# Router logits from unnormalised rows, inside the cross-attention output projection, with the norm factor taken per token

## Chip, cores and metric

One core of one Trainium2 chip. The metric is device microseconds of one execution. The kernel before was timed in three runs; its profile is of a fourth execution. Everything is float32 unless said otherwise.

## Reference

A model of two blocks on 256 tokens of width 1024. The first block is attention and a product-key retrieval of single-neuron experts; the second is convolution and a gated recurrence, cross attention over a memory, and a mixture of experts. The change touches the seam between the last two:

```python
x = x + memory_cross_attention(h, mem_n, w_q, w_k, w_v, w_o)   # ... @ w_o last
h = rms_norm(x, norm_ffn_g)          # x * rsqrt(mean(x*x) + EPS) * g
x = x + hierarchical_moe(h, ...)
return rms_norm(x, final_norm_g)

def hierarchical_moe(h, ...):
    group_probs = softmax(t @ w_group + b_group)         # 4 groups
    g_p, g_idx = top_k(group_probs, 1)
    e_logits = t @ w_expert + b_expert                   # 4 x 8 experts
    e_p, e_idx = top_k(softmax(e_logits of that group), 2)
    weights = g_p * e_p / sum(e_p)
    expert_ids = g_idx * 8 + e_idx
    for e in range(32):
        hid = silu(t @ w_gate[e]) * (t @ w_up[e])        # 1024 -> 512
        y = y + combine[:, e:e + 1] * (hid @ w_down[e])  # 512 -> 1024
```

## The kernel before, in words

The program is one long `build` with a block for each engine: TensorE (PE), VectorE (DVE), ScalarE (ACT), GpSimd (POOL), and the queue engine SP, which issues the loads. The order on each engine is the order of the code, and semaphores join them. x lies transposed as `Xv` (128 features x 8 blocks x 256 tokens). `TT` is 2 tiles of 128 tokens, `KT` 8 blocks of 128 features.

*Weights before the experts* stream through a ring of four slots, each a pair of 1024-column units (1 MB); SP loads pair n when pair n-4 is used (L409 to L423). `project` (L1186) makes one unit of output, 128 features x 256 tokens, from 8 matmuls of a 128x128 stationary tile and 256 streamed columns; each float32 matmul is two passes in the records. The eight units of the cross-attention output (`xo`, L1304) go to banks 0 to 3 in turn, and VectorE adds each to x (L1856, `x4_ready`).

*The router stretch* comes next. ScalarE squares each block of x (L790), PE sums them over features with a matrix of ones (L1308), ScalarE takes the root (L792), VectorE its reciprocal (L1860) and writes the normalised rows h into `Hv` (L1863). PE makes the logits, tokens on partitions, with h as the stationary tile and the 36 router columns streamed (L1315), then turns h and x to token-major form, one 128x128 block at a time (L1325); ScalarE copies the turned banks to `h_tok` and `x_tok` (L795). VectorE adds the bias (L1868), picks the group and two experts (L1869 to L1894), waits for ScalarE's two exponentials (L802, L803), makes the weights `w12` (L1898 to L1901), and one-hot rows `chosen` and `weight` over 32 experts (L1903 to L1911). PE counts each token's place among its expert's tokens (L1330 to L1334) and zeroes the four accumulator banks 0 to 3 by matmuls (L1340). VectorE computes the number of rounds, which every engine reads into a register (L1914 to L1922).

*The expert loop* has 16 pairs of experts a round; 64 slots for each expert; one round is enough when no expert has over 64 tokens. For each pair VectorE makes a one-hot selection `sel` (`one_hot`, L1925); PE gathers the rows of h by it (`gather`, L1344, 32 passes), ScalarE copies them (`take_gathered`, L813), PE does gate and up (`gate_up`, L1360, through `both`, L1357), then turns, down and, one pair later, `scatter` (L1369). The weights of a pair are 12.6 MB. Pair 0's are loaded during the second block (L416 to L420 and L445 to L447), the gates of pair 1 after the last `xo` unit (L449 to L451); from there SP waits for `gate_mm`, `up_mm` and `down_mm` of the pair before (L455 to L462), so each load starts when PE has used what its buffer held.

*The end*: after the last scatter VectorE adds x (L1970), ScalarE squares and roots, VectorE normalises (L1975), SP stores.

Of the kernel before, what the change touches and what calls it, by code (L numbers as in the profile page):

```python
# [19 lines left out]
ALU = mybir.AluOpType  # L20
# [4 lines left out]
P = 128  # L25
# [70 lines left out]
for _n, _w in (("b_mod", 48), ("norm1_g", 8), ("norm2_g", 8), ("final_norm_g", 8), ("norm_mix_g", 8),  # L96
# [16 lines left out]
    "squares_ready": (("sq1_ready", 2), ("sqg_ready", 5), ("sqo_ready", 2), ("sq2_ready", 8), ("sqm_ready", 1), ("sqx_ready", 8), ("sqh_ready", 2), ("sqc_ready", 1), ("sqn_ready", 8), ("sq5_ready", 8)),  # L113
    "deviation_ready": (("std1_ready", 1), ("stdg_ready", 3), ("stdo_ready", 2), ("std2_ready", 1), ("stdm_ready", 1), ("stdx_ready", 2), ("stdc_ready", 1), ("stdh_ready", 2), ("stdn_ready", 1), ("std5_ready", 1), ("std6_ready", 2)),
    "sums_ready": (("ss1_ready", 1), ("ssg_ready", 3), ("sso_ready", 2), ("ss2_ready", 1), ("ssm_ready", 1), ("ssx_ready", 1), ("meanc_ready", 1), ("varc_ready", 1), ("ssh_ready", 2), ("ssn_ready", 1), ("ss5_mm", 1)),
    "h_ready": (("h_x_ready", 8), ("H3_ready", 8), ("H4_ready", 8), ("H5_ready", 8)),
    "x_ready": (("x1_ready", 8), ("x2_ready", 8), ("x2n_ready", 8), ("x3_ready", 8), ("x4_ready", 8)),
# [14 lines left out]
def build(nc, t):  # L132

    ctx = ExitStack()
    with ctx:
# [174 lines left out]
        sq5, rs5 = three(area(4096, 2048), KT), area(6144, 256)  # L310
# [24 lines left out]
        ss5, ri5 = rr[:, 24:26], rr[:, 26:28]  # L335
        cmp4 = rr[:, 28:32]
# [52 lines left out]
        def _(sp):  # L389
# [19 lines left out]
            for m in range(RING, PAIRS2):  # L409
# [4 lines left out]
                if m in (6, 24, 26):  # L414

                    i = {6: 2, 24: 0, 26: 1}[m]  # L416
                    if m == 24:
                        second_done(sp, *BETWEEN[-1])
                    sp.dma_start(w_exp[0][:, 4096 * i:4096 * (i + 1)], t[("moe_gate", "moe_up", "moe_down")[i]][0]).then_inc(
                        S(("gates_in0", "ups_in", "downs_in")[i]), 16)  # L420
                if m == 12:
                    sp.dma_start(r_w.rearrange("p k n -> p (k n)"), t["router_w"]).then_inc(S("router_in"), 16)
                    sp.dma_start(r_b, t["router_b"].broadcast_to([P, 36])).then_inc(S("router_in"), 16)  # L423
# [77 lines left out]
        def _(act):  # L501
# [166 lines left out]
            for b in range(BLOCKS):  # L668
# [11 lines left out]
                if h == 0 and s == 14:  # L680
                    act.wait_ge(S("mem_in"), 16)
# [111 lines left out]
            def take_rows(rows, turned, done, n, b):  # L793
                act.wait_ge(S(turned), n + 1)
                act.activation(rows[:, n // 2, (n % 2) * 512:(n % 2 + 1) * 512], bank[b][:], ACT.Copy).then_inc(S(done), 1)  # L795

            for n in range(4):
                take_rows(h_tok, "h_turned", "h_tok_ready", n, n)
            for n in range(2):
                take_rows(x_tok, "x_turned", "x_tok_ready", n, 4 + n)  # L800
# [3 lines left out]
            for n in range(2, 4):  # L804
                take_rows(x_tok, "x_turned", "x_tok_ready", n, 4 + n % 2)
# [28 lines left out]
            for tt in range(TT):  # L834
                act.wait_ge(S("x5_ready"), 2 * tt + 2)
                act.activation(y_slot, x5[:, tt, :], ACT.Square, accum_out=ss5[:, tt:tt + 1]).then_inc(S("ss5_ready"), 1)
                act.wait_ge(S("ss5_ready"), tt + 1)
# [4 lines left out]
        def _(pe):  # L842
# [461 lines left out]
            project([("xo", i) for i in range(8)], xo)  # L1304

            for k in range(KT):
                pe.wait_ge(S("sq5_ready"), base("sq5_ready") + k + 1)
                last = nc.tensor.matmul(bank[6][:, 0:T], ones, sq5[:, k, :], start=(k == 0), stop=(k == KT - 1))  # L1308
            last.then_inc(S("ss5_mm"), 1)
            pe.wait_ge(S("x4_ready"), base("x4_ready") + 8)  # L1310
            pe.wait_ge(S("H5_ready"), base("H5_ready") + KT)
            pe.wait_ge(S("router_in"), 32)
            for tt in range(TT):
                for k in range(KT):
                    last = nc.tensor.matmul(bank[7][:, 36 * tt:36 * tt + 36], Hv[:, k, tt * P:(tt + 1) * P], r_w[:, k, :],  # L1315
                                            start=(k == 0), stop=(k == KT - 1))
            last.then_inc(S("logits_mm"), 1)
            for src, ready in ((Hv, "h_turned"), (Xv, "x_turned")):
                for n in range(4):
                    b = n if src is Hv else 4 + n % 2  # L1320
                    if src is Xv and n >= 2:
                        pe.wait_ge(S("x_tok_ready"), n - 1)
                    for j in range(4):
                        k = 4 * (n % 2) + j
                        last = nc.tensor.transpose(bank[b][:, j * P:(j + 1) * P], src[:, k, (n // 2) * P:(n // 2 + 1) * P], ident)  # L1325
                    last.then_inc(S(ready), 1)
# [3 lines left out]
            nc.tensor.matmul(bank[6][:, 0:32], before, chosen[:, 0, :], start=True, stop=True)  # L1330
            nc.tensor.matmul(bank[6][:, 32:64], ones, chosen[:, 0, :], start=True, stop=False)
            nc.tensor.matmul(bank[6][:, 32:64], before, chosen[:, 1, :], start=False, stop=True)
            nc.tensor.matmul(bank[6][:, 64:96], ones, chosen[:, 0, :], start=True, stop=False)
            nc.tensor.matmul(bank[6][:, 64:96], ones, chosen[:, 1, :], start=False, stop=True).then_inc(S("places_mm"), 1)  # L1334

            pe.wait_ge(S("h_tok_ready"), 4)
            pe.wait_ge(S("x_tok_ready"), 4)
# [3 lines left out]
            pe.wait_ge(S("rounds_ready"), 1)  # L1341
            n = pe.value_load(rounds[0:1, :], min_val=1, max_val=4)

            def gather(q):  # L1344
# [6 lines left out]
                last.then_inc(S("gather_mm"), 1)  # L1351

# [47 lines left out]
            with pe.Fori(0, n) as r:  # L1400
                q0 = r * 16
                gather(q0)
# [21 lines left out]
                scatter(q0 + 15, True).then_inc(S("round_done"), 1)  # L1424

# [3 lines left out]
        def _(dve):  # L1429
# [322 lines left out]
            dve.wait_ge(S("masks_in"), 16)  # L1752
# [78 lines left out]
            dve.wait_ge(S("x2n_ready"), base("x2n_ready") + KT)  # L1831
            for i in range(8):
# [25 lines left out]
            dve.memset(zeros, 0.0).then_inc(S("zeros5_ready"), 1)  # L1858
            dve.wait_ge(S("std5_ready"), base("std5_ready") + 1)
            link(dve.reciprocal(rs5, rs5))  # L1860
            dve.wait_ge(S("x4_ready"), base("x4_ready") + 8)
# [226 lines left out]
```

## Time and profile before

| | us |
|---|---|
| three runs | 1823.63, 1824.20, 1826.87 |
| their median | 1824.20 |
| the profiled execution | 1826.29 |
| its span in the trace | 1824.2 |
| PE busy in the span | 1480.9 (81%) |
| VectorE busy | 870.0 (48%) |
| ScalarE busy | 522.7 (29%) |
| mean DMA rate | 313 GB/s |

The span runs from the first to the last instruction in the trace; the execution's own time holds something around it. Positions below are microseconds from the span's start. A PEclk of 1.00 is TensorE at its full 2.4 GHz, 0.50 is 1.2 GHz. In brackets stands the idle time of an engine before a row, and what ended it. "issue" is idle time for which the profile shows no releaser.

### The profile page before, as it was taken

The numbers are of one execution on the slowest core, as the hardware profiler recorded it, in microseconds if no ns is written. First come the engines' busy times: TensorE is split into PE (matmuls) and PEld (weight loads), VectorE is DVE, ScalarE is ACT, GpSimd is POOL, SyncE is SP. The second block draws the span as 40 slices with busy tenths as digits, with TensorE's granted clock in tenths as the row PEclk, the third lists the DMA queues.
The fourth block names the chain that finished last, engine by engine and source line by source line (L and its number), as shares of the span: only waits on it lengthen the run. The fifth ranks groups of instructions, "written<-read, shape, count | busy, mean of one in ns | idle before, by whom it ended". The sixth has DMA issues, their size and how long they took to land.

```text
span 1824.2 us, 20361 instructions
## 1 busy us (share of the span) xinstructions
PE 1480.9 (81%) x7580; PEld 899.9 (49%) x7580; DVE 870.0 (48%) x1974; ACT 522.7 (29%) x1317; POOL 282.8 (16%) x277
## 2 busy tenths in 40 slices
PE   8898997666667676666666889998989999999997
PEld 5487686222323232232222789887754544444443
DVE  1777725776666575747444887422222111121212
ACT  2213603444333433433334137302121111111111
POOL 0000001443343434343342000000000000000000
PEclk9999988888878888888798999999989999999998
DMA  8671034999999999999996434363429999999993
GB/s 363 231 278 68 1 113 169 407 425 415 425 390 415 407 412 417 421 425 423 420 427 267 172 104 155 121 225 116 185 118 430 431 431 431 431 431 431 431 419 141
DMA packets 65453, 571.31 MB, mean 313 GB/s; under 512 B 7520, under 2 KB 7776, under 8 KB 8416
## 3 DMA queue, kind: packets, MB, share of 16 engines
q0 software_dynamic: 39312, 286.28, 38.1%
q1 hardware_dynamic: 25344, 281.13, 37.8%
q10 hardware_dynamic: 720, 2.89, 0.4%
q8 instruction: 46, 0.75, 0.2%
q14 instruction: 31, 0.25, 0.0%
HBM read 569.22 MB, written 1.05 MB: 313 GB/s over the span
## 4 chain that ended last, share of the span: by engine, by line
PE 49%; DMA 32%; DVE 9%; issue 5%; ACT 3%; POOL 2%; SPq 0%; POOLq 0%; DVEq 0%; ACTq 0%
DMA big<-in_peer_dram,big 17%; DMA big<-in_moe_up_dram 14%; PE bank L1357 9%; PE bank L1200 8%; PE bank L1074 6%; PE bank L901 4%; PE bank L1021 2%; PE bank L905 2%; POOL big L496 2%; PE bank L1004 2%; PE bank L1265 2%; PE bank L860 1%; PE bank L1226 1%; PE bank L1183 1%; PE bank L1180 1%
## 5 line engine op out<-in xcount | busy, mean ns | idle before, releaser
L1074 PE MATMUL bank<-big 128*64 128x512 f32 x1024 | 319.9, 760 | 228.6 <-ACT big L649 228.1
L496 POOL DMA_INDIRECT big<-in_peer_dram,big x256 | 273.4, 1068 | 572.2 <-PE bank L1074 351.9
L1074 PEld LDWEIGHTS bank<-big 128*64 128x64 f32 x1024 | 75.5, 164 | 424.0 <-ACT big L649 312.5
L1357 PE MATMUL bank<-big 128*64 128x512 f32 x768 | 169.5, 594 | 15.8 <-DMA big<-in_moe_up_dram 14.5
L643 ACT ACTIVATE big<-big 128x1 f32<-128x1 f32 x256 | 51.9, 203 | 394.8 <-DVE misc L1651 195.6
L1651 DVE SCALAR_TENSOR_TENSOR misc<-big 128x1024 f32<-128x1024 f32 x64 | 78.5, 1226 | 95.6 <-DMA big<-in_peer_dram,big 94.4
L1357 PE MATMUL bank<-big,misc 128*64 128x512 f32 x512 | 113.4, 594 | 9.7 <-ACT big L816 9.2
L1357 PEld LDWEIGHTS bank<-big 128*64 128x64 f32 x768 | 58.8, 137 | 123.9 <-issue 98.6
L1651 DVE SCALAR_TENSOR_TENSOR big<-big 128x1024 f32<-128x1024 f32 x64 | 78.6, 1229 | 80.1 <-DMA big<-in_peer_dram,big 78.9
L1200 PE MATMUL bank<-H,ring 128*128 128x256 f32 x448 | 99.1, 384 | 9.6 <-DVE H L1711 6.7
L1651 DVE SCALAR_TENSOR_TENSOR misc<-big,misc 128x1024 f32<-128x1024 f32 x64 | 78.4, 1225 | 43.0 <-DMA big<-in_peer_dram,big 42.7
L1651 DVE SCALAR_TENSOR_TENSOR big<-big,misc 128x1024 f32<-128x1024 f32 x64 | 78.4, 1225 | 41.6 <-DMA big<-in_peer_dram,big 41.2
L1200 PEld LDWEIGHTS bank<-H,ring 128*128 128x128 f32 x448 | 86.1, 193 | 22.7 <-issue 10.9
L1943 DVE TENSOR_TENSOR X<-misc,bank 128x512 f32<-128x512 f32 x16 | 11.0, 688 | 179.7 <-PE bank L1357 179.7
L649 ACT ACTIVATE big<-misc,big 128x64 f32<-128x64 f32 x256 | 89.0, 348 | 8.4
L1953 DVE SCALAR_TENSOR_TENSOR big_parts<-bank,misc,big_parts 128x512 fp32r<-128x512 f32 x32 | 22.5, 746 | 116.5 <-ACT big_parts L823 116.5
L646 ACT ACTIVATE big<-big 128x1 f32<-128x1 f32 x256 | 75.4, 294 | 8.4
L1357 PEld LDWEIGHTS bank<-big,misc 128*64 128x64 f32 x512 | 41.9, 137 | 70.9 <-issue 57.8
L816 ACT ACTIVATE big<-bank 128x512 f32<-128x512 f32 x32 | 17.4, 594 | 199.1 <-PE bank L1349 199.1
L901 PE MATMUL bank<-big,ring 128*128 128x256 f32 (+1 forms) x208 | 64.5, 472 | 5.3 <-ACT big L537 5.3
L1021 PE MATMUL bank<-H,ring 128*128 128x256 f32 x256 | 64.7, 410 | 3.5 <-ACT H L601 3.5
L1021 PEld LDWEIGHTS bank<-H,ring 128*128 128x128 f32 x256 | 52.2, 210 | 18.6 <-issue 11.1
(376 smaller groups left out, 2240.7 us busy)
## 6 DMA issues: line engine op xcount, KB each, us to landing
big<-in_moe_down_dram SPq DMA_DIRECT2D x32, 2048.0 KB, 13.0
big<-in_moe_up_dram SPq DMA_DIRECT2D x32, 2048.0 KB, 17.0
ring<-in_first_dram SPq DMA_DIRECT2D x37, 1024.0 KB, 7.4
ring<-in_second_dram SPq DMA_DIRECT2D x36, 1024.0 KB, 4.8
big<-in_moe_gate_dram SPq DMA_DIRECT2D x16, 2048.0 KB, 15.6
ring<-in_moe_gate_dram SPq DMA_DIRECT2D x16, 2048.0 KB, 15.6
misc<-in_mod_rest_dram POOLq DMA_DIRECT2D x16, 1024.0 KB, 5.6
big<-in_peer_dram,big POOLq DMA_INDIRECT x256
```

The costliest lines, as they stand in the source:

```text
L496: pool.indirect_dma_start(out=gathered[b % GATHERS], out_offset=None, in_=t["peer"], in_offset=bass.IndirectOffsetOnAxis(ap=rows[:, b:b + ...
L643: link(act.activation(acts[:, c], dots[:, c], ACT.Gelu))
L646: link(act.activation(weights[:, c], acts[:, c], ACT.Copy, scale=gate_r[:, c]))
L649: act.activation(diag[:, b % DIAGS, :], pair_ident, ACT.Copy, scale=weights[:, c]).then_inc(S("diag_ready"), 1)
L901: last = nc.tensor.matmul(b[:, 0:n], w[:, k, :], hAll[:, k, a:a + n], start=(k == 0), stop=(k == KT - 1))
L905: last = nc.tensor.matmul(b[:, tt * P:(tt + 1) * P], hAll[:, k, tt * P:(tt + 1) * P], w[:, k, :], start=(k == 0), stop=(k == KT - 1))
L1004: last = nc.tensor.matmul(b[:, 0:T], w[:, k, :], oT[:, k, :], start=(k == 0), stop=(k == KT - 1))
L1021: last = nc.tensor.matmul(bank[4][:, 0:T], w[:, k, :], Hv[:, k, :], start=(k == 0), stop=(k == KT - 1))
L1074: last = nc.tensor.matmul(bank[2 * tt + half][HALF * g:HALF * (g + 1), :], diag[:, b % DIAGS, :], gathered[b % GATHERS][:, a:a + 512], sta ...
L1200: last = nc.tensor.matmul(b[:, 0:T], w[:, k, :], rhs[:, k, :], start=(k == 0), stop=(k == KT - 1))
L1357: last = nc.tensor.matmul(out[c, :], slots[:, c], weights[a], start=(k == 0), stop=(k == n - 1))
L1651: dve.scalar_tensor_tensor(products[b % 2], gathered[b % GATHERS][:, 0:UNIT], 1.0, x_pairs[b // PTOP % TT][:, b % 2, :], ALU.mult, ALU.mul ...
```

## The change

Between the units of `xo`, PE turns the blocks of x that are already final to token-major form, into banks 4 to 7, and before the last unit it makes six of the eight steps of the router logits, now straight from x: the 36 router columns are the stationary tile and 256 tokens are streamed. The gain `norm_ffn_g` is multiplied into the router weights beforehand (VectorE, ahead of the mix additions). ScalarE squares the turned rows with a running sum, so the norm factor comes as one number for each token, in two halves; VectorE applies it to the logits after PE has turned those. `h_tok` is no longer turned from h, but made by VectorE from `x_tok`, the factor and the gain along the rows (`ffn_g`, a new 512 KB load). The one-hot rows of chosen experts are made first; the weights, the rounds and the exponentials' sums come behind the first one-hot selection. The gather of pair 0 is issued before PE reads the number of rounds, and a gather for the next round stands at the end of each.

ScalarE:

```diff
-            for k in range(KT):
-                act.wait_ge(S("x4_ready"), base("x4_ready") + k + 1)
-                act.activation(sq5[:, k, :], Xv[:, k, :], ACT.Square).then_inc(S("sq5_ready"), 1)
-            act.wait_ge(S("ss5_mm"), base("ss5_mm") + 1)
-            act.activation(rs5, bank[6][:, 0:T], ACT.Sqrt, scale=1.0 / D, bias=eps).then_inc(S("std5_ready"), 1)
...
+            take_turned(0, first5)
+            copy_turned(0)
+            act.activation(spare5[:, 0:1], eps, ACT.Sqrt)
+            take_turned(1, second5)
+            act.wait_ge(S("bias5_ready"), 1)
+            for tt in range(TT):
+                act.wait_ge(S("ss5_tok"), 3 + tt)
+                act.activation(ss5[:, tt:tt + 1], second5[:, tt:tt + 1], ACT.Sqrt, scale=1.0 / D, bias=bias5[:, tt:tt + 1]).then_inc(S("std5_ready"), 1)
+            act.activation(spare5[:, 1:2], eps, ACT.Exp)
+            copy_turned(1)
```

`take_turned(half, sums)` waits for `x_turned` and squares two banks of 128x512 with `accum_out`; `copy_turned(half)` copies them to `x_tok` (`x_tok_ready`).

PE:

```diff
-            project([("xo", i) for i in range(8)], xo)
-            for k in range(KT):
-                last = nc.tensor.matmul(bank[6][:, 0:T], ones, sq5[:, k, :], start=(k == 0), stop=(k == KT - 1))
...
+            def turn_tokens(k):
+                pe.wait_ge(S("x4_ready"), base("x4_ready") + k + 1)
+                for tt in range(TT):
+                    last = nc.tensor.transpose(bank[4 + 2 * tt + k // 4][:, (k % 4) * P:(k % 4 + 1) * P], Xv[:, k, tt * P:(tt + 1) * P], ident)
+                if k % 4 == 3:
+                    last.then_inc(S("x_turned"), 1)
+            def route(k):
+                if k == 0:
+                    pe.wait_ge(S("x_tok_ready"), 2)
+                    pe.wait_ge(S("router_scaled"), 1)
+                last = nc.tensor.matmul(bank[4][0:36, 0:T], r_w[:, k, :], Xv[:, k, :], start=(k == 0), stop=(k == KT - 1))
...
+            project([("xo", 0)], xo)
+            for i in range(1, 7):
+                project([("xo", i)], xo)
+                turn_tokens(i - 1)
+            for k in range(6):
+                route(k)
+            project([("xo", 7)], xo)
+            for k in (6, 7):
+                turn_tokens(k)
+                route(k)
             pe.wait_ge(S("zeros5_ready"), 1)
             for b in range(4):
                 nc.tensor.matmul(bank[b][:], zeros[:, 0:P], zeros, start=True, stop=False, skip_group_check=True)
+                if b == 0:
+                    pe.wait_ge(S("logitT_ready"), 1)
+                    for tt in range(TT):
+                        last = nc.tensor.transpose(bank[6][:, 36 * tt:36 * tt + 36], logitT[0:36, tt * P:(tt + 1) * P], ident[0:36, 0:36])
+                    last.then_inc(S("logits_turned"), 1)
...
+            pe.wait_ge(S("h_tok_ready"), base("h_tok_ready") + 1)
+            pe.wait_ge(S("x_tok_ready"), 4)
+            gather(0)
+            pe.wait_ge(S("rounds_ready"), 1)
+            n = pe.value_load(rounds[0:1, :], min_val=1, max_val=4)
...
             with pe.Fori(0, n) as r:
                 q0 = r * 16
-                gather(q0)
...
                 scatter(q0 + 15, True).then_inc(S("round_done"), 1)
+                gather(q0 + 16)
```

The place matmuls stand after the zero matmuls, in bank 4. VectorE:

```diff
+            dve.tensor_tensor(r_w, r_w, each(v("norm_ffn_g", 0, 8), 36), ALU.mult).then_inc(S("router_scaled"), 1)
...
+                if i == 6:
+                    dve.wait_ge(S("ss5_tok"), 2)
+                    dve.tensor_scalar(bias5, first5, 1.0 / D, EPS, ALU.mult, ALU.add).then_inc(S("bias5_ready"), 1)
...
-            link(dve.reciprocal(rs5, rs5))
-            for k in range(KT):
-                dve.scalar_tensor_tensor(Hv[:, k, :], Xv[:, k, :], v("norm_ffn_g", k), rs5, ALU.mult, ALU.mult).then_inc(S("H5_ready"), 1)
+            dve.tensor_copy(logitT[0:36, :], bank[4][0:36, 0:T]).then_inc(S("logitT_ready"), 1)
+            dve.wait_ge(S("std5_ready"), base("std5_ready") + 2)
+            link(dve.reciprocal(ri5, ss5))
+            dve.wait_ge(S("logits_turned"), 1)
+            for tt in range(TT):
+                turned, r = bank[6][:, 36 * tt:36 * tt + 36], ri5[:, tt:tt + 1]
+                dve.scalar_tensor_tensor(g8[:, tt, 0:GROUPS], turned[:, 0:GROUPS], r, r_b[:, 0:GROUPS], ALU.mult, ALU.add)
...
+                ins = dve.scalar_tensor_tensor(logit[:, tt, :], turned, r, r_b, ALU.mult, ALU.add)
...
-            dve.wait_ge(S("exp5_ready"), 1)
             dve.wait_ge(S("eid_ready"), 1)
...
             dve.tensor_tensor(chosen, chosen, oh, ALU.add).then_inc(S("chosen_ready"), 1)
+            dve.wait_ge(S("x_tok_ready"), 4)
+            for tt in range(TT):
+                ins = dve.scalar_tensor_tensor(h_tok[:, tt, :], x_tok[:, tt, :], ri5[:, tt:tt + 1], ffn_g, ALU.mult, ALU.mult)
+            ins.then_inc(S("h_tok_ready"), 1)
             dve.wait_ge(S("places_mm"), 1)
+            link(dve.tensor_copy(place, three(bank[4][:, 0:64], TT)))
...
+            one_hot(sel, chosen, 0).then_inc(S("sel_ready"), 1)
+            link(dve.reduce_max(most, bank[4][:, 64:96], AX))
...
+            dve.wait_ge(S("exp5_ready"), 1)
+            link(dve.reduce_sum(gsm, gex, AX))
...
                 dve.wait_ge(S("place_moved"), r + 1)
+                one_hot(sel, chosen, 0).then_inc(S("sel_ready"), 1)
```

SP loads the gain after unit pair 32: `sp.dma_start(ffn_g, t["ffn_g"].broadcast_to([P, D]))`, into the gate buffer's third quarter, free by then.

## Rows read from the trace of the kernel before

**Rows 1.** Chain of waits, 1280 to 1440: start us, length us, what.

```profile
...
1288.07 27.89 PE bank L1200 x128
1315.97 3.45 PE bank L1308 x16
1319.42 5.69 issue
1325.11 7.01 PE bank L1315 x32
...
1352.94 13.95 PE bank L1357 x64
...
```

**Rows 2.** Busy time by stretch: length, busy us per engine, PEclk, DMA share, GB/s.

```profile
...
1331.00:1360.00 29.00, 23.95 (x122) 15.80 (x123) 9.28 (x55) 9.69 (x15) 0.00 (x0) 0.86 0.00 1
1360.00:1420.00 60.00, 58.78 (x310) 28.48 (x305) 10.46 (x28) 9.06 (x13) 0.00 (x0) 1.00 0.99 418
1420.00:1770.00 350.00, 328.16 (x1707) 160.55 (x1704) 62.80 (x168) 50.78 (x72) 0.00 (x0) 1.00 1.01 431
...
```

**Rows 3.** Order of time around the mix and xo additions: start us, us, engine, line.

```profile
...
1207.51 0.42 DVE L1834 TENSOR_TENSOR X<-bank,X 128x256 f32<-128x256 f32 x1 [3.88 <-PE bank L1200]
...
1315.59 3.43 PEld L1308 LDWEIGHTS bank<-big,const 128*128 128x128 f32 x16
...
1316.00 0.80 SPq L430 DMA_DIRECT2D ring<-in_moe_gate_dram  x2
1316.00 0.43 DVE L1856 TENSOR_TENSOR X<-bank,X 128x256 f32<-128x256 f32 x1 [3.03 <-PE bank L1200]
...
```

**Rows 4.** Order of time, four turns in the expert loop.

```profile
...
1370.39 0.47 PEld L1385 LDWEIGHTS bank<-const,X 128*128 128x128 f32 x4
...
```

**Rows 5.** ScalarE's forms by line: xcount: duration ns min/median/max, starts.

```profile
...
L795 ACT ACTIVATE big<-bank x8: 577/597/598, 1333.1 to 1339.3; 128x512 f32<-128x512 f32 x8
...
L781 ACT ACTIVATION_READ_ACCUMULATOR big<-bank,misc x8: 192/196/200, 1269.7 to 1275.9; 128x1 f32 x8
...
L838 ACT ACTIVATE misc<-misc x2: 294/294/294, 1817.8 to 1819.2; 128x1 f32<-128x1 f32 x2
...
```

**Rows 6.** Order of time, from the selection to gate and up of pair 0.

```profile
...
1332.69 0.24 DVE L1871 MAX8 big<-big 128x8 f32<-128x8 f32 x2
...
1335.41 0.17 DVE L1894 SCALAR_TENSOR_TENSOR misc<-misc 128x4 f32<-128x4 f32 x1
...
1339.00 0.16 DVE L1898 TENSOR_REDUCE misc<-big 128x2 f32<-128x8 f32 x1 [3.42 <-ACT misc L803]
...
1339.79 0.24 DVE L1903 TENSOR_SCALAR misc<-const,misc 128x32 f32<-128x32 f32 x1
...
1341.32 0.23 DVE L1910 TENSOR_TENSOR misc<-misc,big 128x64 f32<-128x64 f32 x1
...
1341.60 0.41 PE L1330 MATMUL bank<-misc,const 128*128 128x32 f32 x2 [3.54 <-DVE misc L1910]
...
1343.00 0.17 DVE L1914 TENSOR_SCALAR misc<-const 128x4 f32<-128x4 f32 x1 [1.32 <-PE bank L1334]
...
1345.19 0.98 DVE L1930 TENSOR_SCALAR big<-const,misc 128x64 f32<-128x64 f32 x4 [1.15 <-issue]
...
1347.52 0.19 PEld L1349 LDWEIGHTS bank<-big 128*128 128x128 f32 x1 [0.24 <-issue]
...
1351.72 1.09 ACT L816 ACTIVATE big<-bank 128x512 f32<-128x512 f32 x2 [5.46 <-PE bank L1349]
...
```

**Rows 7.** VectorE's 128x1024 multiply, by line.

```profile
...
L1975 DVE SCALAR_TENSOR_TENSOR misc<-misc x2: 1285/1286/1286, 1818.4 to 1819.8; 128x1024 f32<-128x1024 f32 x2
...
```

**Rows 8.** Busy time by stretch, columns as rows 2: the two stretches at half clock.

```profile
...
1322.20:1335.90 13.70, 10.79 (x51) 10.82 (x52) 5.81 (x32) 2.08 (x4) 0.00 (x0) 0.50 0.48 202
...
1342.70:1346.10 3.40, 3.40 (x6) 1.56 (x6) 1.85 (x10) 1.12 (x1) 0.00 (x0) 0.50 0.00 0
...
```

**Rows 9.** Order of time, the last expert pair's end.

```profile
...
1814.06 2.48 DVE L1970 TENSOR_TENSOR misc<-bank,big 128x512 f32<-128x512 f32 x4 [3.65 <-PE bank L1377]
...
```

More of the change, by code:

```diff
@@ L309, in build @@
         h_tok, x_tok = three(area(0, 2048), TT), three(area(2048, 2048), TT)
-        sq5, rs5 = three(area(4096, 2048), KT), area(6144, 256)
+        x_turned = [bank[b][:] for b in range(4, 8)]
+        junk5 = three(area(4096, 2048), 4)
+        logitT = area(6144, 256)
+        ffn_g = work[:, 2048:3072]
         hg = three(area(4096, 1024), KT)
@@ L786, in _, with take_turned, copy_turned @@
                 act.activation(xPT[:, h, :, :].rearrange("p k q -> p (k q)"), bank[6 + h % 2][:], ACT.Copy).then_inc(S("xPT_ready"), 1)
[L788 to L800 removed]
+            def take_turned(half, sums):
+                act.wait_ge(S("x_turned"), half + 1)
+                for tt in range(TT):
+                    act.activation(junk5[:, 2 * half + tt, :], x_turned[2 * tt + half], ACT.Square, accum_out=sums[:, tt:tt + 1]).then_inc(S("ss5_tok"), 1)
+            def copy_turned(half):
+                for tt in range(TT):
+                    act.activation(x_tok[:, tt, half * 512:(half + 1) * 512], x_turned[2 * tt + half], ACT.Copy).then_inc(S("x_tok_ready"), 1)
+            take_turned(0, first5)
[8 more added lines that the diff above has]
+            copy_turned(1)
             act.wait_ge(S("shifted5"), 2)
@@ L1313, in _ @@
-            for tt in range(TT):
-                for k in range(KT):
[L1315 to L1326, printed above, removed]
@@ L1328, in _ @@
-            pe.wait_ge(S("chosen_ready"), 1)
-            before = cst("before")
[L1330 to L1334, printed above, removed]
@@ L1340, in _ @@
                 nc.tensor.matmul(bank[b][:], zeros[:, 0:P], zeros, start=True, stop=False, skip_group_check=True)
-            pe.wait_ge(S("rounds_ready"), 1)
-            n = pe.value_load(rounds[0:1, :], min_val=1, max_val=4)
+                if b == 0:
[3 more added lines that the diff above has]
+                    last.then_inc(S("logits_turned"), 1)
+            pe.wait_ge(S("chosen_ready"), 1)
+            before = cst("before")
+            nc.tensor.matmul(bank[4][:, 0:32], before, chosen[:, 0, :], start=True, stop=True)
+            nc.tensor.matmul(bank[4][:, 32:64], ones, chosen[:, 0, :], start=True, stop=False)
+            nc.tensor.matmul(bank[4][:, 32:64], before, chosen[:, 1, :], start=False, stop=True)
+            nc.tensor.matmul(bank[4][:, 64:96], ones, chosen[:, 0, :], start=True, stop=False)
+            nc.tensor.matmul(bank[4][:, 64:96], ones, chosen[:, 1, :], start=False, stop=True).then_inc(S("places_mm"), 1)
+            pe.wait_ge(S("h_tok_ready"), base("h_tok_ready") + 1)
+            pe.wait_ge(S("x_tok_ready"), 4)
             def gather(q):
@@ L1909, in _ @@
+                ins = dve.tensor_scalar(oh[:, tt, :], cst("iota")[:, 0:EXPERTS], eid[:, tt, 1:2], None, ALU.is_equal)
             link(ins)
             dve.tensor_tensor(chosen, chosen, oh, ALU.add).then_inc(S("chosen_ready"), 1)
[L1911 to L1915 removed]
```

92 lines of the change are left out of this document (44 added, 48 removed).

## The prediction

> **What bounds the kernel now.** I read the chain of waits first, cut to the stretch around the change, then busy time by stretch, then the order of time there. The chain [rows 1] runs through TensorE (PE) from the cross-attention output (L1200, 1288.07) through the sum of squares (L1308), 5.69 us of standing still, the logits (L1315) and on to gate and up of expert pair 0 (L1357, 1352.94). Nothing in it is a load. The reader is to see next [rows 2] that from 1331 to 1360 the DMA engines move nothing (1 GB/s), that they restart at 1360, and that from 1420 to 1770 they are full (431 GB/s). So the long last stage is bound by loads of expert weights, but its stream starts only when pair 0 frees its buffers, a fixed distance behind 1352.94. What the router stretch gives up, the whole rest moves forward: the question is the start of gate and up of pair 0, and nothing else.
>
> **The new chain, in profile time.**
> 1. *Projection xo with turns and logits between.* Eight units take 27.6 (1288.07 to 1315.6, where the next weight load starts [rows 1, 3]), 3.45 each. A turn of one 128x128 block is one pass of 0.115: four in 0.47 [rows 4]. A logit step (256 columns, one tile of 36) is a matmul of xo's form: 3.45/8 = 0.43. The trace has no 36-column stationary tile with 256 columns streamed; between 0.22 (the 36-column logits of [rows 1]: 32 passes in 7.01) and 0.43 I take 0.43, for the streamed side is xo's. Ahead of the last unit's end stand 12 turns (1.4) and 6 logit steps (2.6): xo 7 ends at 1315.6 + 4.0 = 1319.6. The logits stand behind the copies of the first half of the tokens (xo 4 done, about 1306.2; two squares and two copies, below 3 us), needed only at 1313.6: 4 us to spare. If that cover went, the wait would be the excess over it.
> 2. *Last X.* X's addition starts 0.4 behind the unit and lasts 0.43 [rows 3]: seen by PE at 1320.55. Turn of block 7: 1320.9.
> 3. *Norm factor.* Two ScalarE squares over 128x512 with a sum: a 128x512 copy is 0.60, a sum's readout 0.20, partly under the next [rows 5], so 0.70 each: 1322.5 with the semaphore. (Bounds 0.60 and 0.80 each: 0.2 either way.) Two square roots of one column, 0.29 each, overlapped: 1323.1; its table was loaded during xo. Reciprocal and four short multiply-adds at some 0.2: 1324.05. The other branch, logits to SBUF (0.42), two turns under the first zero matmul, is there at 1322.5 and waits. In the kernel before this point (start of the first MAX8) is 1332.69 [rows 6]: 8.6 gained.
> 4. *Selection*, unchanged: 1332.69 to 1335.58, 2.9 [rows 6]: 1326.95.
> 5. *Experts chosen ahead of weights.* Gone are VectorE's wait of 3.42 for the exponentials, four short operations (0.8) and four of eight comparisons (the eight: 1339.79 to 1341.32, 0.19 each) [rows 6]. Left: four comparisons 0.8, addition 0.25: chosen at 1328.0. Before, 1341.55: 13.5 gained.
> 6. *Token rows.* Scaling x to h now stands on the path: two 128x1024 multiplies, 1.285 each [rows 7], plus a 0.17 constant: 1330.8. The place matmuls (1341.60 to 1343.00, 1.4 [rows 6]) lie beside it. The copies of the second half of x, behind ScalarE's table load, end near 1325.7 and are needed at 1328.2. Copy of places 0.25, first one-hot 0.98 [rows 6]: 1332.1, where before it was 1346.2.
> 7. *Gather of pair 0.* Then 4.2 from first weight load to ScalarE's copy (1347.52 to 1351.72), and 1.22 to gate and up (1352.94) [rows 1, 6]. At full clock gate and up start at 1337.5, 15.4 earlier.
>
> **Clock.** After PE had stood still 3.54 before L1330, it ran 3.4 us at granted clock 0.50 (1342.7 to 1346.1); after 5.69 idle it ran at 0.50 for 13.7 us, 1322.2 to 1335.9 [rows 1, 6, 8]. 0.50 is 1.2 of the 2.4 GHz. Before, only the zero matmuls and a hidden part paid for the first. Now PE has nothing to do from about 1325 (eight zero passes of 512 columns, 0.43 each by xo's 256 in 0.216, behind the last logit step at 1321.5) to 1328 and from 1329.2 to 1332.1, and the gather comes next. The lower bound of this cost is 0; the upper is 13.7 at half clock, 6.9. I take 3.8 us at half clock, near the 3.54-us case since both gaps are of its size: 1.9. Gate and up start at 1339.4: **13.5 us gained**.
>
> **Edits at nothing.** Rounds, the exponentials' sums and weights run on VectorE behind the one-hot, under gather and gate-up of pair 0 (some 4 us against 18). The scaling of the router weights (128x288, below 0.5) has VectorE's 3.88 idle ahead of the first mix addition [rows 3]. The 512 KB load of the norm gain follows unit pair 32 on SP's queue, while the query projection (xq) runs; behind it stand the loads of xo 2 to 7, three of 1 MB, of which the first is needed at 1288.07 + 2 x 3.45 = 1295, two projections later, and pair 0's second expert. Nothing on that queue waits for it but they. The last gather, for a round that does not come, runs after the last scatter: the one-hot it needs (1.0) lies under PE's final scatter, VectorE standing idle 3.65 there [rows 9], and even twice a gather's 4.2 behind 1814.0 ends at 1822.4, ahead of the span's 1824.2. If it did not fit, the end would come later by the excess.
>
> PE reads the number of rounds after gather 0. VectorE spent 1.15 on read and loop entry [rows 6]; PE's is bounded by 0 and 1.15 here, and ScalarE's copy hides 1.2. I take 0. The Trainium skill ("Runtime: NRT & Kernel Launch", Instruction fetch mechanics) warns that a taken branch outside the prefetched pages stalls until a page is fetched. It names no price; the sum by it is that of the rival below, and no row shows PE entering this loop separately.
>
> **Sum.** The profiled execution took 1826.3 for a span of 1824.2; less 13.5 that is 1812.8. The median of the runs, 1824.2, is 2.1 below the profiled one, and I give the median: **1810.7**. A measurement can tell about 0.2% (3.6 us) from no change.
>
> **Rivals.**
> - *Clock stays up through the gather*: 15.4 gained, 1808.8. For it: two gaps with work between, both under 3.54. Against: 3.54 was enough. Chance 0.10.
> - *Clock stays down* as after L1308: the loss is up to 6.9, 8.5 gained, 1815.7. For it: the gaps together are 5.9. Against: what ran in the 13.7 us was half short 36-column matmuls; a gather is dense. 0.15.
> - *PE's loop entry is exposed*: PE's read and branch take two to three times VectorE's 1.15, less the 1.2 hidden: 1.1 to 2.3 later, 1811.8 to 1813.0. The skill's rule speaks for it; PE's 0.24 between zeros and gather before, against. 0.06.
> - *No gain, weights bound throughout*: then the end does not move, 1824.2. Against: DMA idle 1331 to 1360 [rows 2]. 0.04.
> - *Slower*: SP issues pair 1's gate weights when xo 7 is done (1316.00 [rows 3]), now 4.0 later. If the stream is continuous from this load on, the end moves back 4.0: 1828.2. It decides once those weights (1331 now, 1335 then) land after pair 1 needs them; that is at 1339.4 + 18, so 20 us of slack speak against. 0.03.
>
> **Numbers.** The forecast holds 0.62. Range 1807.5 to 1815.5: the warm case less a microsecond of run scatter at one end, the cold case at the other; what lies outside (no gain, slower, part of the cold case) is below 2 in 10. Faster 0.93, same 0.04, slower 0.03.
>
> **What would show it.** xo 7 near 1319.6 with turns between units; first MAX8 near 1324; chosen near 1328 with no wait for the exponentials; first gather load near 1332 with PEclk 0.5 in part; L-line of gate and up near 1339; DMA idle ending near 1347 instead of 1360, and 431 GB/s for as long as before. I would be wrong if gate and up start before 1337 or after 1345, or if the DMA-full stretch grows longer than it was.

## The result and the profile after

The changed kernel took 1807.5 us (median of four runs, 1804.4 to 1807.6), the kernel before 1823.9 (four runs). The measured ratio is 0.9896, interval 0.9882 to 0.9909. Put on the 1824.2 that the prediction started from, that is 1805.2: faster, as forecast, and 2.3 below the range of 1807.5 to 1815.5. The two medians alone divide to 0.9910, which is 1807.8 and just inside the range; nothing here shows where the 0.0014 (2.6 us) between the two figures comes from, and the miss is no larger than that. One later run of the changed kernel, in e2, took 2258.5 us at a mean granted clock of 0.64 and is in no comparison. The profiled executions have spans of 1824.2 and 1805.5.

The chain of waits of the changed kernel, from 1280 to 1365, answers to [rows 1]:

```profile
...
1285.50 7.17 PE bank L1212 x32
1292.90 3.46 PE bank L1212 x16
...
1311.27 2.71 PE bank L1327 x12
1313.98 3.65 PE bank L1212 x16
...
1318.80 0.73 ACT big L799 x3
...
1321.43 0.25 DVE big L1901 x2
...
1325.07 0.23 DVE misc L1932
...
1326.47 1.28 DVE big L1936
1327.92 1.00 DVE big L1949 x4
1329.06 5.27 PE bank L1366 x32
...
1335.57 13.96 PE bank L1378 x64
...
```

The eight units of xo with turns and logit steps between them are one piece without a gap; the sum of squares, the 5.69 of standing still and the 7.01 of logits are gone. In their place stand short steps on ScalarE and VectorE, the second token-row multiply (1326.47), and the gather (1329.06). From xo's first matmul to gate and up of pair 0 it is 1335.57 - 1285.50 = 50.07, before it was 1352.94 - 1288.07 = 64.87. I call this stretch the *seam*: 14.8 shorter.

Busy time by stretch, which answers to [rows 2] (same columns):

```profile
...
1331.00:1342.80 11.80, 10.54 (x59) 5.70 (x60) 2.37 (x11) 3.35 (x5) 0.00 (x0) 0.95 0.00 0
...
1342.80:1402.00 59.20, 57.98 (x304) 28.24 (x302) 10.47 (x28) 8.96 (x13) 0.00 (x0) 1.00 0.99 417
1402.00:1752.00 350.00, 327.94 (x1708) 160.71 (x1706) 62.82 (x168) 50.78 (x72) 0.00 (x0) 1.00 1.01 431
...
```

The DMA engines stand idle to 1342.8 instead of 1360 and are then full at 431 GB/s for as long as before. As predicted, the stream of expert weights moved forward whole.

In order of time, the steps of the seam, which answer to [rows 3] and [rows 6]:

```profile
...
1317.66 0.80 SPq L438 DMA_DIRECT2D ring<-in_moe_gate_dram  x2
...
1318.33 0.44 PE L1319 MATMUL bank<-const,X 128*128 128x128 f32 x2
...
1320.47 0.17 DVE L1891 RECIPROCAL misc<-misc 128x2 f32<-128x2 f32 x1 [0.69 <-ACT misc L812]
...
1321.43 0.24 DVE L1901 MAX8 big<-big 128x8 f32<-128x8 f32 x2
...
1325.07 0.23 DVE L1932 TENSOR_TENSOR misc<-misc,big 128x64 f32<-128x64 f32 x1
...
1325.28 2.48 DVE L1936 SCALAR_TENSOR_TENSOR big<-big,misc 128x1024 f32<-128x1024 f32 x2
...
1325.35 0.41 PE L1352 MATMUL bank<-misc,const 128*128 128x32 f32 x2 [1.96 <-DVE misc L1932]
...
1327.67 0.22 DVE L1941 COPY misc<-bank 128x64 f32<-128x64 f32 x1
1327.92 0.98 DVE L1949 TENSOR_SCALAR big<-const,misc 128x64 f32<-128x64 f32 x4
...
1329.02 5.09 PEld L1366 LDWEIGHTS bank<-big 128*128 128x128 f32 x32 [2.49 <-issue]
...
1334.34 1.08 ACT L828 ACTIVATE big<-bank 128x512 f32<-128x512 f32 x2 [2.47 <-PE bank L1366]
...
```

The reader is to see that VectorE has no wait between 1320.47 and the end of the multiplies (L1936), that the second multiply and not the place matmuls (L1352 on) ends last before the copy of the places (L1941), and that the gather runs from 1329.02 to ScalarE's copy at 1334.34, 5.3.

### The profile page after: what moved, and what is told of

Its sections match the earlier page's. It is cut to its first block, busy times and chain, and to the rows that moved or that the text cites. A ratio compares the mean times of both kernels' runs of the same rounds, so it can differ in the third digit from the quotient of the medians.

```text
span 1805.5 us, 20337 instructions
## 1 busy us (share of the span) xinstructions
PE 1482.5 (82%) x7566; PEld 896.1 (50%) x7566; DVE 868.9 (48%) x1977; ACT 519.7 (29%) x1316; POOL 286.4 (16%) x277
## 4 chain that ended last, share of the span: by engine, by line
PE 49%; DMA 33%; DVE 9%; issue 5%; ACT 4%; POOL 1%; SPq 0%; POOLq 0%; DVEq 0%; ACTq 0%
DMA big<-in_peer_dram,big 17%; DMA big<-in_moe_up_dram 14%; PE bank L1378 9%; PE bank L1212 8%; PE bank L1086 7%; PE bank L913 4%; PE bank L1033 2%; PE bank L917 2%; PE bank L1016 2%; PE bank L1277 2%; PE bank L872 1%; POOL big L504 1%; PE bank L1238 1%; PE bank L1366 1%; PE bank L1195 1%
## 5 line engine op out<-in xcount | busy, mean ns | idle before, releaser
L1212 PE MATMUL bank<-H,ring 128*128 128x256 f32 x448 | 102.6, 393 | 9.6 <-DVE H L1732 6.7
L1212 PEld LDWEIGHTS bank<-H,ring 128*128 128x128 f32 x448 | 88.6, 198 | 23.7 <-issue 10.9
L1378 PEld LDWEIGHTS bank<-big,misc 128*64 128x64 f32 x512 | 41.9, 137 | 70.9 <-issue 57.8
L1033 PE MATMUL bank<-H,ring 128*128 128x256 f32 x256 | 67.0, 420 | 3.5 <-ACT H L609 3.5
L1366 PE MATMUL bank<-big 128*128 128x128 f32 x544 | 65.1, 279 | 2.4 <-DVE big L1949 2.4
```

Of the source, the lines that this page charges most:

```text
L1033: last = nc.tensor.matmul(bank[4][:, 0:T], w[:, k, :], Hv[:, k, :], start=(k == 0), stop=(k == KT - 1))
L1212: last = nc.tensor.matmul(b[:, 0:T], w[:, k, :], rhs[:, k, :], start=(k == 0), stop=(k == KT - 1))
L1366: last = nc.tensor.matmul(bank[6 + k // 4][:, (k % 4) * P:(k % 4 + 1) * P], h_tok[:, tt, k * P:(k + 1) * P], sel[:, tt, :], start=(tt == 0 ...
L1378: last = nc.tensor.matmul(out[c, :], slots[:, c], weights[a], start=(k == 0), stop=(k == n - 1))
```

## How the experiments are read

Each profile was cut in the same way: *retrieval* from the first dot product to the first sum of squares behind the retrieval, *middle* from there to xo's first matmul, the *seam*, *experts* from there to the addition behind the last scatter, and the *rest* behind it. What lies ahead of the first dot product (305.2 to 309.4 us in the fourteen profiles) is not in the table. The two profiles shown so far differ by 18.7, of which the seam has 14.8. The starts of the first instruction of each stretch give (us):

```
                          retrieval  middle   seam  experts   rest
before                        686.0   293.6   64.9    461.2   10.1
e1  before, again             685.6   296.0   64.7    459.9   10.1
e9  before, again             680.9   295.4   66.0    460.1   10.2
e11 before, again             682.4   296.1   66.0    460.2   10.1
after                         681.5   295.8   50.1    459.8   10.1
e2  after, again              684.6   296.1   50.1    461.2   10.1
e10 after, again              685.9   295.5   50.0    461.0   10.1
e12 after, again              685.0   295.9   50.1    461.1   10.1
e3  after, weights first      683.6   296.7   52.8    460.6   10.2
e4  before, weights late      683.0   295.6   60.6    459.4   10.2
e5  after, logits late        684.0   295.8   50.0    461.1   10.1
e6  after, filled             684.6   295.5   48.6    460.4   10.1
e7  after, no last gather     683.1   296.0   50.4    460.9   10.1
e8  attempt at better         682.2   296.0   47.8    460.0   10.1
```

The experts differ by up to 1.8, and that is TensorE's clock at their end. The last scatter, eight passes, took 3.66 in the first profile of the kernel before (from 1810.37, at a granted clock of 0.54) and 2.14 in that of the changed kernel (from 1793.18, at 1.00); over all fourteen profiles it took 2.1 to 3.7, in both kernels. Without it the experts took 457.2 to 457.9 everywhere. So the 1.3 by which the experts of the first two profiles differ is this clock, and not the change.

## Experiments: is the rest of the gain the change's?

Both kernels were run again unchanged, on two chips, with two theories: *A*, all outside the seam is scatter of single executions; *B*, the change moves the stages before and behind it.

e1, the kernel before:

> The kernel before once more, for a second profile. Theory A (the 2.6 us by which xo began earlier in the changed kernel's profile, and the 1.5 us between the last scatter and the final addition, are scatter of single executions): xo begins somewhere within 1283 to 1290, first xo matmul to first gate-and-up matmul is 64.9 +- 0.5, and the stretch from the first gate-and-up matmul to the span's end is anywhere between 469.5 and 471.5. Theory B (the change moves them): xo begins at 1288 +- 0.5 and the last stretch is 471.3 +- 0.3 again. Time 1822 to 1827 by both.

Ratio to before 1.0003 (0.9991 to 1.0015), 1820.6 to 1830.7 in 12 runs. Seam 64.7; experts 459.9, which is what B reserved for the changed kernel (with the rest 470.0, where B wanted 471.3 here). xo began at 1288.1, which both had allowed. For A.

e2, the changed kernel:

> The changed kernel once more. Theory A: xo to gate and up 50.1 +- 1 (the clock at gather 0 may differ), start of xo within 1283 to 1290, last stretch 469.5 to 471.5. Theory B: xo begins at 1285.5 +- 0.5, last stretch 469.9 +- 0.3. Time 1804 to 1808, ratio 0.990 to 0.992.

Ratio 0.9936 (0.9916 to 0.9955), median 1813.4 of five runs; so the time missed what both theories had said (1804 to 1808), and the seam, 50.1, did not. xo begins at 1290.1 instead of 1285.5, at the very edge of what A had allowed, and experts take 461.2, what the kernel before took. Against B.

e9 and e11, the kernel before, and e10 and e12, the changed one, side by side on one chip:

> The kernel before, third profile. Seen so far in both kernels and variants: retrieval stretch (first dot product to first sum of squares of x2) 681.5 to 686.0, from there to xo 293.6 to 296.7, first gate-and-up matmul to final addition 459.4 to 461.2. If these scatter by execution and not by kernel, this one lies anywhere within (retrieval below 684.5 about half the time). If the kernel before is slower there by itself, retrieval is 685.5 or more again. Seam 64.8.

> The changed kernel, third profile. By execution: retrieval anywhere from 681.5 to 686; by kernel: 684.6 or less. Seam 50.1. Time ratio to before, from the seam alone: 1 - 14.7/1824 = 0.9919, with 0.992 inside the interval if nothing else moves.

> The kernel before, fourth profile: as e9. By execution the retrieval stretch lies anywhere from 681.5 to 686; by kernel it is 685.5 or more. Seam 64.8.

> The changed kernel, fourth profile: as e10. By execution the retrieval stretch lies anywhere from 681.5 to 686; by kernel it is 684.6 or less. Seam 50.1.

Ratios 0.9992 (0.9982 to 1.0002) and 1.0000 (0.9987 to 1.0014) for before; 0.9906 (0.9887 to 0.9925) and 0.9925 (0.9908 to 0.9943) for the changed kernel. The retrieval took 680.9 and 682.4 in the kernel before, where B wanted 685.5 or more, and 685.9 and 685.0 in the changed kernel, where B wanted 684.6 or less; B is out. The 680.9 is also 0.6 below all that A had allowed (681.5 to 686.0). The mean over four profiles each is 683.7 before and 684.3 after. The seam of before is not quite fixed: 66.0 twice. In e9 the chain has the zero matmuls at 6.12, against 5.15 in the first profile, the clock being down for longer (granted 0.51 from 1334.8 to 1341.6, 6.8 us, against the 3.4 us of [rows 8]):

```profile
...
1281.53 27.89 PE bank L1200 x128
...
1336.60 6.12 PE bank L1340 x8
...
```

So the seam is 65.4 on the mean of four, against 50.1: 15.3, or a ratio of 1 - 15.3/1824 = 0.9916. The four ratios of the changed kernel, 0.9896, 0.9936, 0.9906 and 0.9925, have the mean 0.9916. That the two agree to the last digit is luck: the medians of the same runs divide to 0.9910, 0.9941, 0.9910 and 0.9932, mean 0.9923, or 1.3 us less gain. Within this scatter nothing is left over for another part of the change.

## Experiments: the parts of the seam

**e3, weights first.** The weights put back ahead of the chosen rows:

```diff
             oh, ohw = three(scr[:, 0:64], TT), three(scr[:, 72:136], TT)
+            dve.wait_ge(S("exp5_ready"), 1)
+            link(dve.reduce_sum(gsm, gex, AX))
...
+            link(dve.tensor_tensor(weight, weight, ohw, ALU.add))
             for tt in range(TT):
                 dve.tensor_scalar(chosen[:, tt, :], ...)
```

> The changed kernel with the wait for the exponentials and the weights put back ahead of the chosen rows. My step 5: the exponentials are there at 1324.4, ScalarE no longer being late, so the wait costs about 0.2; four short operations 0.8, four comparisons and one addition 1.1: chosen, and all behind it, 2.1 later than in e2. Rival (the wait itself of 3.42 is what was saved): 4.5 later than e2, or more.

```profile
...
1325.94 0.16 DVE L1929 TENSOR_REDUCE misc<-big 128x2 f32<-128x8 f32 x1 [0.16 <-ACT misc L817]
...
1328.66 0.23 DVE L1942 TENSOR_TENSOR misc<-misc,big 128x64 f32<-128x64 f32 x1
...
1332.64 5.86 PE L1366 MATMUL bank<-big 128*128 128x128 f32 x32 [2.40 <-DVE big L1959]
...
```

The wait for the exponentials is 0.16, not 3.42. Chosen ends at 1328.89, 41.9 behind xo's start (1287.0); in e2 it was 39.8: 2.1 later, as my step 5 has it. The gather starts with the clock down for longer (5.86 instead of 5.27), which makes it 2.7 for the seam. The rival, 4.5 or more, is out. The time, 0.9938 (0.9922 to 0.9954), can't be told from e2's 0.9936: a few microseconds are only seen in the seam. In the kernel before, then, 3.4 of what the order gained was ScalarE being late with copies ahead of its table load; in the changed kernel the copies are done in time, and the order itself is worth 2.1 and its clock.

**e4, only the order, in the kernel before.** The wait and the weights go behind the number of rounds:

```diff
-            dve.wait_ge(S("exp5_ready"), 1)
             dve.wait_ge(S("eid_ready"), 1)
-            link(dve.reduce_sum(gsm, gex, AX))
...
             dve.tensor_tensor(chosen, chosen, oh, ALU.add).then_inc(S("chosen_ready"), 1)
...
             dve.tensor_copy(rounds, rnd).then_inc(S("rounds_ready"), 1)
             dve.wait_ge(S("rounds_ready"), 1)
+            dve.wait_ge(S("exp5_ready"), 1)
+            link(dve.reduce_sum(gsm, gex, AX))
...
```

> The kernel before with only this order changed: chosen rows made first, weights behind the rounds. Chosen comes 4.7 earlier (1336.9), but PE then waits for ScalarE's last copy of x (x_tok, 1339.9, itself behind the exponentials) before the zero matmuls and gather: 2.7 us gained, ratio 0.9985. Rival (the order alone carries its full 4.7): 0.9974. Rival (nothing, since the zero matmuls run as late as before): 1.000.

```profile
...
1332.42 0.23 DVE L1902 TENSOR_TENSOR misc<-misc,big 128x64 f32<-128x64 f32 x1
...
1334.46 1.06 ACT L795 ACTIVATE big<-bank 128x512 f32<-128x512 f32 x2
...
1335.62 3.67 PE L1340 MATMUL bank<-misc 128*128 128x512 f32 x8 [0.94 <-issue]
...
1338.66 0.98 DVE L1930 TENSOR_SCALAR big<-const,misc 128x64 f32<-128x64 f32 x4 [0.90 <-issue]
...
1339.69 3.84 PE L1349 MATMUL bank<-big 128*128 128x128 f32 x32 [0.40 <-DVE big L1930]
...
```

Seam 60.6, 4.2 less than the first two profiles of before and 4.8 less than the mean of four; ratio 0.9968 (0.9955 to 0.998). I had expected 2.7 us and 0.9985, which is outside the interval; the rival with the full 4.7 (0.9974) is inside. Chosen is 4.7 earlier in the changed order, and PE waits for ScalarE's copies (done at 1335.52) before the zero matmuls, as I had said: they start 51.4 behind xo's start instead of 54.7. What I missed is that PE's idle time is then short, and the eight zero passes take 3.67 instead of 5.34: full clock. The order is 4 to 5 of the 15. The other 10 (e2 against e4: 50.1 against 60.6) came with the rest of the change together: norm factor for each token, logits straight from x, h made from x, turns of x between the units. The runs take only the interleaved logits (e5) out of it; what the turns are worth alone was not run.

**e5, logits late.** All eight steps behind xo 7:

```diff
-            for k in range(6):
-                route(k)
             project([("xo", 7)], xo)
             for k in (6, 7):
                 turn_tokens(k)
-                route(k)
+            for k in range(8):
+                route(k)
```

> The changed kernel with all eight logit steps behind xo 7. My sum puts six of them, 2.6 us, on the path ahead of xo 7 and holds that the norm factor, not the logits, ends the seam's front. Then xo 7 ends 2.6 earlier, the norm factor is there 2.6 earlier, the last logit step ends where it did, and the logits (copy and turns) come last: the first MAX8 is 0.5 earlier to 0.3 later against xo's start than in e2, the seam 49.5 to 50.5. Rival (interleaving the logits is what the change gained): seam 52.6.

```profile
...
1318.78 0.42 DVE L1888 COPY big<-bank 36x256 f32<-36x256 f32 x1 [4.08 <-PE bank L1327]
1319.12 0.15 DVE L1890 RECIPROCAL misc<-misc 128x2 f32<-128x2 f32 x1
...
1320.14 0.35 DVE L1894 SCALAR_TENSOR_TENSOR big<-bank,misc 128x4 f32<-128x4 f32 x2 [0.88 <-PE bank L1346]
...
1320.85 0.24 DVE L1900 MAX8 big<-big 128x8 f32<-128x8 f32 x2
...
```

The square roots are done before the last logit step, and VectorE now waits 0.88 for the turned logits (L1346) instead of for the norm factor. First MAX8 1320.85 - 1285.0 = 35.85 behind xo's start, in the changed kernel 35.93. Seam 50.0. The rival, 52.6, is out: the interleaving of the logits is worth nothing here. What is left for them is that they are made from x before its norm is known, which no run takes away by itself. Ratio 0.9916 (0.9903 to 0.9929).

**e6, filled.** PE is kept busy where it stood still:

```diff
+            pe.wait_ge(S("x_tok_ready"), 4)
+            for _ in range(2):
+                nc.tensor.matmul(bank[5][:], ident, x_tok[:, 0, 0:512], start=True, stop=True)
             pe.wait_ge(S("chosen_ready"), 1)
...
+            for _ in range(2):
+                nc.tensor.matmul(bank[5][:], ident, x_tok[:, 0, 0:512], start=True, stop=True)
             pe.wait_ge(S("h_tok_ready"), base("h_tok_ready") + 1)
-            pe.wait_ge(S("x_tok_ready"), 4)
```

> The changed kernel with two 512-column matmuls into the unused bank 5 ahead of the place matmuls and two behind them (their result is not used), so that PE does not stand still for 2 to 2.5 us twice. If the clock drop comes from this idle time, gather 0 takes 3.8 to 4.2 from its first weight load to the copy instead of 5.3, and the seam is 48.9. Rival (the clock falls for what the window held before, or the fillers run past the one-hot): seam 50 or more.

In the changed kernel the clock by stretch is this (columns as rows 2):

```profile
...
1323.40:1329.00 5.60, 1.30 (x10) 1.19 (x10) 5.39 (x22) 0.30 (x2) 0.00 (x0) 0.97 1.01 429
1329.00:1332.60 3.60, 3.54 (x19) 3.58 (x20) 2.25 (x13) 1.28 (x1) 0.00 (x0) 0.57 0.38 154
1332.60:1334.40 1.80, 1.71 (x16) 1.51 (x14) 0.00 (x0) 0.06 (x1) 0.00 (x0) 1.00 0.00 0
...
```

PE is busy 1.3 of the 5.6 us before the gather, still at a granted clock near 1.00; 0.57 is granted over the first 3.6 of the gather, 1.00 after. In the filled kernel:

```profile
...
1324.64 1.88 PE L1352 MATMUL bank<-big,const 128*128 128x512 f32 x4
...
1327.90 1.96 PE L1362 MATMUL bank<-big,const 128*128 128x512 f32 x4
...
1330.47 3.81 PE L1370 MATMUL bank<-big 128*128 128x128 f32 x32 [0.60 <-DVE big L1953]
...
1334.31 1.08 ACT L828 ACTIVATE big<-bank 128x512 f32<-128x512 f32 x2 [1.03 <-PE bank L1370]
...
```

The gather's 32 passes take 3.81, from first load to copy 3.9 instead of 5.3; the seam is 48.6, 1.5 shorter. The second pair of fillers (1.96) ends just before the one-hot. Ratio 0.9906 (0.9891 to 0.9921), within the four of the changed kernel: not to be told apart by time.

**e7, no last gather** (it leaves out what a second round would need):

```diff
                 scatter(q0 + 15, True).then_inc(S("round_done"), 1)
-                gather(q0 + 16)
...
                 dve.wait_ge(S("place_moved"), r + 1)
-                one_hot(sel, chosen, 0).then_inc(S("sel_ready"), 1)
```

> The changed kernel without the gather and one-hot at the end of a round (it leaves out what a second round would need; there is one round here). My prediction costed them at nothing: first gate-and-up matmul to the final addition 459.4 to 461.4 as in all profiles so far, final addition to the span's end 10.1. Rival (the last gather holds back the end, or the one-hot the final addition): end 9.5 or less, or the former stretch shorter than 459.4.

Experts 460.9, rest 10.1, ratio 0.9928 (0.9915 to 0.994): no gain. (The seam's 50.4 is the clock again, the gather taking 5.62 here.) In the changed kernel, where they are, the end reads

```profile
...
1793.26 0.98 DVE L1949 TENSOR_SCALAR big<-const,misc 128x64 f32<-128x64 f32 x4
...
1795.15 3.74 PE L1366 MATMUL bank<-big 128*128 128x128 f32 x32
1795.35 2.48 DVE L2007 TENSOR_TENSOR misc<-bank,big 128x512 f32<-128x512 f32 x4 [1.11 <-PE bank L1398]
...
```

The one-hot (L1949) is over before PE's last scatter, VectorE still waits for PE 1.1 before the additions, and the gather runs beside them. That VectorE waited 3.65 there in [rows 9] and 1.11 here is the one-hot itself (0.98) and the last scatter, 3.66 there and 2.14 here, as said above.

**e8, an attempt at better.** The norm factor goes into the one-hot rows (chosen times `ri5`), so the token rows need only the gain; half of that multiply is made beside xo, half beside the place matmuls; with fillers, two and one:

```diff
+                    dve.wait_ge(S("x_tok_ready"), 2)
+                    dve.wait_ge(S("router_in"), 48)
+                    dve.tensor_tensor(h_tok[:, :, 0:512], x_tok[:, :, 0:512], wide(ffn_g[:, 0:512], TT), ALU.mult)
...
-                ins = dve.scalar_tensor_tensor(h_tok[:, tt, :], x_tok[:, tt, :], ri5[:, tt:tt + 1], ffn_g, ALU.mult, ALU.mult)
+            dve.tensor_tensor(h_tok[:, :, 512:D], x_tok[:, :, 512:D], wide(ffn_g[:, 512:D], TT), ALU.mult).then_inc(S("h_tok_ready"), 1)
...
+            dve.tensor_tensor(chosen_r, chosen, each(ri5, EXPERTS), ALU.mult)
-            one_hot(sel, chosen, 0).then_inc(S("sel_ready"), 1)
+            one_hot(sel, chosen_r, 0).then_inc(S("sel_ready"), 1)
```

> An attempt at a better kernel: the norm factor multiplied into the one-hot rows instead of the token rows, so that the gain's multiply is one half beside xo (VectorE idle there) and one half, 1.3, beside the place matmuls; and fillers, two and one. One-hot ready 0.8 earlier, gather 1.2 shorter: seam 48.0. Rival (the place matmuls bound that stretch already, and the clock falls anyway): seam 50.

```profile
...
1313.23 1.22 DVE L1894 TENSOR_TENSOR big<-big,misc 128x1024 f32<-128x1024 f32 x1
...
1327.01 1.22 DVE L1943 TENSOR_TENSOR big<-big,misc 128x1024 f32<-128x1024 f32 x1
...
1328.41 0.22 DVE L1947 TENSOR_TENSOR big<-misc 128x64 f32<-128x64 f32 x1 [0.19 <-PE bank L1360]
...
1328.81 0.98 DVE L1956 TENSOR_SCALAR big<-const,misc,big 128x64 f32<-128x64 f32 x4
...
1329.94 3.81 PE L1371 MATMUL bank<-big 128*128 128x128 f32 x32 [0.62 <-DVE big L1956]
...
```

One multiply of 1.22 is on the path, where two took 2.48; only 0.9 of the difference of 1.3 is gained, as VectorE now waits 0.19 for the place matmuls and has one short operation more. The gather starts at 1329.94 - 1287.2 = 42.7 behind xo's start instead of 43.6, and takes 3.8. Seam 47.8, the shortest of all: 2.3 less than the changed kernel. Its ratio is 0.9898 (0.9883 to 0.9912), its median the lowest of those beside it (1806.2; e5 1808.3, e6 1808.1), but the intervals overlap with those of the changed kernel, whose own four ratios go from 0.9896 to 0.9936. That it is faster is shown by the seam, not by the time of whole runs.

## Why the prediction was right, and where it was wrong

The mechanism held; the step that failed is the lower end of the range, its "microsecond of run scatter", and two terms of the sum were too large.

*Right.* That the start of gate and up of pair 0 is all that counts: experts took 459.4 to 461.2 in all fourteen profiles, wherever they began, and 457.2 to 457.9 without the last scatter. That the weights' stream would move with it. The steps, each counted from xo's first matmul:

```
                                     predicted   changed kernel
gate weights of pair 1 issued             31.9             32.2
last X turned (start)                     32.5             32.8
first MAX8                                36.0             35.9
chosen rows ready                         39.9             39.8
token rows ready                          42.7             42.3
first load of the gather                  44.0             43.5
gather, first load to copy                 6.1              5.3
copy to gate and up                        1.2              1.2
gate and up                               51.3             50.1
```

By the prediction's own sign of being wrong, gate and up before 1337, the first profile fails with 1335.57. But that sign was in profile time, and xo began 2.6 earlier there: counted from xo it is 1338.1. e2, e10 and e12 have 1340.2, 1339.2 and 1339.7. A position behind 1280 us of other work is no test of a stretch; its distance from xo is.

The edits at nothing cost nothing: the last gather (e7), the reading of the rounds behind gather 0 (1.2 from copy to gate and up, as before), the gain's load (the middle took 295.5 to 296.1 with it and 293.6 to 296.1 without, in four profiles each), and the router weights' multiply (0.45, in VectorE's idle time).

*Wrong, first: the term for the clock.* "I take 3.8 us at half clock ... 1.9." Gather and clock together took 5.3 and not 6.1. The clock's share is 1.4 to 1.5, not 1.9, as e6 has the same gather at full clock in 3.9; the rest is that the 4.2 taken from the kernel before was 0.3 too much for such a gather. It is a real cost and of this cause: with PE kept busy it vanishes (e6). The kernel before paid the same cost in another place: its zero matmuls took 4.9 to 6.1 in the chain where e4 shows 3.7 at full clock. The sum had this in it, as it starts from the measured 1352.94, but as a fixed thing; it moves between executions, and that is why the seam of before is 64.7 to 66.0.

*Second: step 6.* The two multiplies with their constant took 2.5, not 2.75: the second began 0.1 before the first had ended, and the constant cost no time. With the link behind them and the 0.1 by which chosen came earlier, the gather's first load is 0.5 earlier. Together the seam came out 1.3 shorter than predicted on the profile I worked from, 1.8 on the mean of four.

*Third, and what put the result outside: the range.* "The warm case less a microsecond of run scatter at one end." The warm case (1808.8) was in the range; the scatter was mis-sized. Three runs had shown 1823.6 to 1826.9, and I read one microsecond from them. Over 11 to 23 runs each the kernel before goes from 1818.6 to 1831.4, and the changed kernel's ratio, for one and the same kernel, came out as 0.9896, 0.9906, 0.9925 and 0.9936. Those four scatter by 0.0018 (standard deviation), 3.3 us. The mean, 0.9916, is 1808.9 on 1824.2, and in the range. The first measurement, 0.9896, is 3.6 us below that mean: that part no mechanism of the change explains. Of the four ratios two lie in the range (0.9925 and 0.9936) and two below it (0.9896 and 0.9906, the bound being 0.9908). So which side a single measurement fell on was chance; that the bound stood too near to the mean was the mistake.

The rivals: the clock staying down as after L1308 (up to 6.9 lost) did not happen; an exposed loop entry did not either (1.2 from copy to gate and up). "Weights bound throughout" and "slower" fail with the experts' constant length. The closest in number was the first, the clock staying up (15.4 gained), but by luck, for the clock did drop: where it stayed up, in e6, the seam was 16.3 shorter than in the first profile of before (64.9 and 48.6).

*What stays open.* Why the retrieval differs by 5 us between executions of the same kernel, and the work ahead of it by 4 (305.2 to 309.4). It wasn't tried: it is outside of the change. Also open is where the measured ratio of 0.9896 and the 0.9910 of the medians part.

## What to carry to other kernels

Where a long stage is bound by a stream that starts a fixed distance behind one event, count everything from that event and the microseconds ahead of it go through one to one. A row norm between a matmul and its consumer can be taken off the path when it is a factor for each token: make the product from the unnormalised rows and apply the factor to the small result, or put it into the next one-hot. Before giving a range, ask how much a stage of scattered DMA alone moves between executions: for gains below 1% a stretch cut out of the profile tells what whole runs can't.

## What the runs showed of the hardware

- The same retrieval code took 680.9 to 686.0 in fourteen profiles, at 410 to 412 GB/s in the eight profiles of the two kernels.
- TensorE's clock can be held up by matmuls whose result is not used: 3.81 instead of 5.27 for the same 32 passes; without them there are gaps of 1.96 and 2.41 us, with PE busy 1.3 of 5.6. In e4 the zero matmuls took 3.67, with a gap of 1 us right before them; in the kernel before, with 3.54 idle ahead of the place matmuls, they took from 5.05 (e1) to 6.30 (e9) in order of time, the gap being 3.54 in both.
- The last scatter's eight passes took 2.10 to 3.66 in fourteen profiles, with the same 2.23 us of waiting ahead of them in all (granted 0.54 in the first profile of the kernel before, 1.00 in e1 of the same kernel): one gap gave either clock.
- A step with a stationary tile of 36 columns and 256 streamed took 0.45 (12 passes in 2.71), the price of a full tile's (0.43) and not that of 36 streamed columns (32 passes in 7.01 at half clock, so by estimate 0.22 for two passes at full clock).
